# The last step of three expert stages, written out without the work for a next group of experts

## The chip, the cores and the metric

One core of a Trainium2 chip runs the whole program. The metric is the device time of one execution in microseconds (us), median of the runs. TensorE has a granted clock, 2.4 GHz at 1.0 and 1.2 GHz at 0.5 in the profile's column PEclk.

## The reference

256 tokens of width 1024 go through two blocks. The first has forgetting attention, a state-space branch and a mixture of experts; the second has two layers (a convolution or block attention, attention over a memory of 256 rows, and a mixture of experts each), with layer norms. The three mixtures are the stages e1, e2 and e3. Each has 32 experts, of which every token uses two; e1's experts are 256 wide, those of e2 and e3 512. The reference, cut to one mixture:

```python
def hierarchical_moe(x, w_rg, b_rg, w_re, b_re, w_gate, w_up, w_down):
    ...
    combine = (jax.nn.one_hot(g_idx, N_GROUPS, dtype=jnp.float32)[:, :, None]
               * within[:, None, :]).astype(t.dtype)
    out = jnp.zeros_like(t)
    for g in range(N_GROUPS):
        h = (jax.nn.silu(jnp.einsum('td,edf->tef', t, w_gate[g]))
             * jnp.einsum('td,edf->tef', t, w_up[g]))
        out = out + jnp.einsum('tef,efd->td', h * combine[:, g, :, None], w_down[g])
    return out.reshape(b_, s_, d_)
```

## The kernel before

A stage takes its experts in groups: four at a time in e1 (8 steps), two at a time in e2 and e3 (16 steps). The 128 columns of a matmul's token side are shared out among the experts of a group. A step of a group works like this, in the order of TensorE's program (`step_`, lines 1071 to 1181):

- The gate products, then the up products (line 1125), from `xg`, the gathered tokens of this group, and the weights as they arrive. `arrived` waits for a transfer of weights. In e2 and e3 each expert's matrix comes in two halves of 1 MB, so k = 4 and, for the down weights, f = 2 have a wait of their own; in e1 a matrix is one transfer of 1 MB.
- The gather of the next group's tokens, first half (line 1133, matmuls at line 1032 in e1 and 1045 in e2 and e3) against the one-hot matrix `S` that VectorE has made one step ahead.
- Four transposes (two in e1) of h (line 1136), which VectorE has multiplied together (line 2206) from ScalarE's SiLU (line 1622) and the up products in PSUM.
- The second half of the gather (line 1139), and two transposes of the shares `Sw` (line 1141).
- The down products (line 1164), once ScalarE has copied the turned h to `hT` (line 1626); the first product with f = 0 of each half also waits until the gather's bank has been copied out (`xgA`, ScalarE line 1591; `xgB`, VectorE line 2165), since it writes the same PSUM bank (4 or 7).
- The scatter (line 1177): shares times the result `og` (copied out by lines 1628 and 2213) is added to four banks that hold the sum over all groups.

VectorE makes `S` and `Sw` for the next group (`places` and `shares_of`, lines 2148 to 2163) at the start of its step. After the last group there is no next one; the kernel makes the one-hot, the shares and the gather all the same, for experts 32 and up, whose columns are filled so that they choose nobody, and nothing reads them. Two waits behind the last step (lines 1191 and 1192) see that these copies have ended.

In e1 all steps are written out, on every engine. In e2 and e3 TensorE and ScalarE have a loop of 8 rounds with two steps each; VectorE has its first and its last step outside of a loop of 7 rounds. Semaphores are counted up through all stages: `before_layer` adds what the stages before have counted, and for the five names that run one group ahead one step more per stage.

SyncE issues the weights on one queue: per step gate, up and down, each when the buffer is free (`used`). Behind a stage's last weights it issues the chunks that the next part of the program needs.

Of the kernel before, what the change touches and what calls it, by code (L numbers as in the profile page):

```python
# [38 lines left out]
GROUP = {"e1": 4, "e2": 2, "e3": 2}  # L39
# [59 lines left out]
def _build(ctx, nc, ins, out):  # L99
# [435 lines left out]
    def after(eng, who, name):  # L535

        eng.wait_ge(finished[who], milestones[who].index(name) + 1)
# [1 line left out]

    per_step = {"S": 2, "gathA": 1, "gathB": 1, "xgA": 1, "xgB": 1, "silu": 1, "h": 1, "T": 1, "hT": 1, "Sw": 1, "SwT": 1,  # L540
                "down": 1, "outA": 1, "outB": 1, "scattered_bank": 2, "scattered0": 1, "scattered": 1}
    ahead = ("S", "gathA", "gathB", "xgA", "xgB")

    def before_layer(e, name):

        return sum(per_step[name] * (STEPS[x] + (name in ahead)) for x in GROUP if x < e)


    SEED = 1
# [1 line left out]
    def moe_wait(eng, e, name, value):  # L551

        eng.wait_ge(flag("moe_" + name), value + (before_layer(e, name) + SEED))
# [264 lines left out]
    def _(pe):  # L818
# [135 lines left out]
        def moe(e, tok):  # L954
# [113 lines left out]
                                  start=(k == 0), stop=(k == KD - 1))  # L1068
                close_bank(last, "memv")

            def step_(u, i, keys=False, values=False):

                def c(k, per=1):

                    return i * (2 * per) + (u * per + k)
# [52 lines left out]
                            elif e != "e1" and k % 4 == 3 and n in (1, 3):  # L1128
                                last.then_inc(used[slots[X * g + (n == 1)][0] + k // 4], 1)

                moe_wait(pe, e, "S", c(4, 2))
                moe_wait(pe, e, "outA", c(0))
                gather_parts(1 - u, 0)
                moe_wait(pe, e, "h", c(1))
                for f in range(F):
                    last = pe.transpose(psum[:, 5, f * P:(f + 1) * P], hh[:, f * P:(f + 1) * P], ident[:, :])
                last.then_inc(flag("moe_T"), 1)
                moe_wait(pe, e, "outB", c(0))
                gather_parts(1 - u, 1)
                for th in range(TH):  # L1140
                    last = pe.transpose(psum[:, 6, th * P:(th + 1) * P], Sw[:, u, th, :], ident[:, :])
                last.then_inc(flag("moe_Sw"), 1)
# [5 lines left out]
                for fs, half in ([(range(F), 0), (range(F), 1)] if e == "e1" else  # L1148
                                 [((0, 1), 0), ((0, 1), 1), ((2, 3), 0), ((2, 3), 1)]):
                    if 0 in fs:  # L1150
                        moe_wait(pe, e, ("xgA", "xgB")[half], c(2))
                    elif half == 0:
                        for x in range(X):
                            arrived(2 * X + x, 1)
                    for f in fs:
                        for n in blocks:
                            r = slice(n * BLOCK, (n + 1) * BLOCK)
                            if e == "e1":
                                w = wv[n][:, f, half * 512:(half + 1) * 512]
                            elif n:  # L1160
                                w = wv[n == 1][:, f, half * 512:(half + 1) * 512]
                            else:
                                w = ring_flat[:, bass.ds(chosen + (4 * SLOT + f * D + half * 512), 512)]
                            last = mm(psum[r, (4, 7)[half], :], hT[:, f, r], w, start=(f == 0), stop=(f == F - 1))  # L1164
                            if half and f == fs[-1] and (e == "e1" or n in (1, 3)):
                                hs = slots[2 * X + (n if e == "e1" else n == 1)][0]
                                last.then_inc(used[hs + (f == 3)], 1)
                    if half == 0 and F - 1 in fs:
                        last.then_inc(flag("moe_down"), 1)
# [12 lines left out]

            if e == "e1":
                for n in range(STEPS[e]):
                    step_(n % 2, n // 2, n == KEYS_AT, n == VALUES_AT)
            else:
                with pe.Fori(0, STEPS[e] // 2) as i:
                    for u in range(2):
                        step_(u, i)

            moe_wait(pe, e, "xgA", STEPS[e] + 1)
            moe_wait(pe, e, "xgB", STEPS[e] + 1)


            ovp, ovv = flag(e + "_ovf_pe"), flag(e + "_ovf_vec")
            after(pe, "vec", e + "_items")
# [348 lines left out]
    def _(ac):  # L1545
# [38 lines left out]
        def moe(e):  # L1584
            S, Sw, SwT, xg, sg, hT = tiles[e]
            F = 2 if e == "e1" else 4
            FW = F * P
            X = GROUP[e]

            def gathered(par):  # L1590
                act(xg[:, par, 0:4, :], psum[:, 4, :].rearrange("p (k c) -> p k c", k=4), ACT.Copy).then_inc(flag("moe_xgA"), 1)  # L1591

            after(ac, "vec", e + "_gd")
            step(act(r_ge, r_gd, ACT.Exp))
            finish(ac, "act", e + "_ge")
            after(ac, "vec", e + "_d21")
            step(act(r_p2, r_d21, ACT.Exp))
            finish(ac, "act", e + "_p2")
            if e != "e1":
                for th in range(TH):  # L1600
                    step(act(parts[0][th], x_sb[:, th, :], ACT.Copy))
                finish(ac, "act", e + "_hi")
            if e != "e3":
                src = full(ac, e + "sums")
                copy_out((e + "sums",), wr_sums[:, :], src[:, 0:2 * NR])
            moe_wait(ac, e, "gathA", 1)
            gathered(0)
            if e == "e1":
                ac.dma_start(wr[:, :, :], ins["wr"][2]).then_inc(flag("router_w3"), 16)
            if e != "e1":  # L1610
                for th in range(TH):
                    after(ac, "vec", e + f"_rest{th}")
                    step(act(parts[1][th], rest[th], ACT.Copy))
                    finish(ac, "act", e + f"_mid{th}")
            def step_(u, i):

                def c(k, per=1):
                    return i * (2 * per) + (u * per + k)

                hs, per, at_u = last_half(e, u, X - 1)  # L1620
                ac.wait_ge(used[hs], i * per + (moe_used[e][hs] + at_u + 1 + SEED))
                act(sg[:, 0:FW], psum[:, 5, 0:FW], ACT.Silu).then_inc(flag("moe_silu"), 1)  # L1622
                moe_wait(ac, e, "gathA", c(2))
                gathered(1 - u)
                moe_wait(ac, e, "T", c(1))
                act(hT[:, 0:F, :], psum[:, 5, 0:FW].rearrange("p (f c) -> p f c", f=F), ACT.Copy).then_inc(flag("moe_hT"), 1)
                moe_wait(ac, e, "down", c(1))
                act(og[:, 0:512], psum[:, 4, :], ACT.Copy).then_inc(flag("moe_outA"), 1)  # L1628

            if e == "e1":  # L1630
                for n in range(STEPS[e]):
                    if n == KEYS_AT:
                        src = full(ac, "memk")
                        copy_out(("memk",), mem_k[:, :, :], src.rearrange("p (a t) -> p a t", a=2))
                    step_(n % 2, n // 2)
            else:
                with ac.Fori(0, STEPS[e] // 2) as i:
                    for u in range(2):
                        step_(u, i)
            after(ac, "vec", e + "_items")  # L1640
            n = ac.value_load(ovf[0:1, 2 * NOVF:2 * NOVF + 1], min_val=0, max_val=ITEMS[e])
            with ac.If(n > 0):
                with ac.Fori(0, n) as k_:
                    ac.wait_ge(flag(e + "_ovf_pe"), k_ * OVF_PE + (OVF_PE + 2))
                    act(sg[:, 0:FW], psum[:, 5, 0:FW], ACT.Silu).then_inc(flag(e + "_ovf_silu"), 1)
# [234 lines left out]
    def _(ve):  # L1880
# [194 lines left out]
        def moe(e):  # L2075
# [118 lines left out]
                    step(tt(parts[2][th], rest[th], parts[1][th], ALU.subtract))  # L2194
                tell(e + "_parts")

            def step_(u, n, i, first=False):

                places(1 - u, n + 1)
                shares_of(1 - u, n + 1)  # L2200
                if first and e != "e1":
                    thirds()
                hs, per, at_u = last_half(e, u, 2 * X - 1)
                ve.wait_ge(used[hs], i * per + (moe_used[e][hs] + at_u + 1 + SEED))
                moe_wait(ve, e, "silu", n + 1)
                tt(hh[:, 0:FW], sg[:, 0:FW], psum[:, 6, 0:FW], ALU.mult).then_inc(flag("moe_h"), 1)  # L2206
                moe_wait(ve, e, "gathB", n + 2)
                gathered(1 - u)
                moe_wait(ve, e, "Sw", n + 1)
                ve.tensor_copy(SwT[:, :], psum[:, 6, 0:T]).then_inc(flag("moe_SwT"), 1)  # L2210
                hs, per, at_u = last_half(e, u, 3 * X - 1)
                ve.wait_ge(used[hs], i * per + (moe_used[e][hs] + at_u + 1 + SEED))
                ve.tensor_copy(og[:, 512:1024], psum[:, 7, :]).then_inc(flag("moe_outB"), 1)  # L2213
# [32 lines left out]
            if e == "e1":  # L2246
# [8 lines left out]
                for n in range(1, STEPS[e]):  # L2255
                    if n == VALUES_AT:
                        src = full(ve, "memv")
                        read_out(ve.tensor_copy(mem_v[:, :, :], src.rearrange("p (a t) -> p a t", a=2)), "memv")
                    step_(n % 2, n, n // 2)
            else:  # L2260
                with ve.Fori(0, last) as i:
                    step_(1, i * 2 + 1, i)
                    step_(0, i * 2 + 2, i + 1)
                step_(1, STEPS[e] - 1, last)
            ovp, ovv = flag(e + "_ovf_pe"), flag(e + "_ovf_vec")
            n = ve.value_load(ovf[0:1, 2 * NOVF:2 * NOVF + 1], min_val=0, max_val=ITEMS[e])
            with ve.If(n > 0):
# [485 lines left out]
```

## Time and profile before

| | us |
|---|---|
| median of 3 runs | 1691.69 (1689.48 to 1695.86) |
| the profiled execution | 1690.12, of which the span of the instructions 1688.4 |
| TensorE busy | 1589.4 (94% of the span) |
| VectorE, ScalarE, GpSimd busy | 512.8, 276.6, 35.9 |
| mean granted clock of TensorE | 0.986 |
| moved by DMA | 570 MB, 338 GB/s on average |

By the page, the chain of work that ended last is 64% TensorE and 30% one tensor's transfers, the up weights (in_e_up). The busiest lines of TensorE are 1125 (520.5 us) and 1164 (257.2 us). e1 runs from about 245 to 470 us of the span, e2 from 597 to 1061, e3 from 1216 to 1680. A busy TensorE is not a TensorE at its peak, since the ends of matmuls are modelled; what decides is which wait ends last at each place. The rows below are times in us from the start of the span.

### The profile page before, as it was taken

The numbers are of one execution on the slowest core, as the hardware profiler recorded it, in microseconds if no ns is written. First come the engines' busy times: TensorE is split into PE (matmuls) and PEld (weight loads), VectorE is DVE, ScalarE is ACT, GpSimd is POOL, SyncE is SP. The second block draws the span as 40 slices with busy tenths as digits, with TensorE's granted clock in tenths as the row PEclk, the third lists the DMA queues.
The fourth block names the chain that finished last, engine by engine and source line by source line (L and its number), as shares of the span: only waits on it lengthen the run. The fifth ranks groups of instructions, "written<-read, shape, count | busy, mean of one in ns | idle before, by whom it ended". The sixth has DMA issues, their size and how long they took to land.

```text
span 1688.4 us, 30942 instructions
## 1 busy us (share of the span) xinstructions
PE 1589.4 (94%) x12616; PEld 795.9 (47%) x12620; DVE 512.8 (30%) x1162; ACT 276.6 (16%) x549; POOL 35.9 (2%) x78
## 2 busy tenths in 40 slices
PE   7999999876799999999999999999999999999997
PEld 5487765533467544343433333674543434333332
DVE  7994333110157551111111111414631111111113
ACT  2304120000035221000100100214210100010011
POOL 4000000100000000000000000000000000000000
PEclk9999999988899999999999999999999999999999
DMA  6322769999983289999999999841399999999996
GB/s 253 139 112 72 319 253 415 421 421 421 422 334 134 76 347 422 422 421 422 422 422 422 422 422 424 353 148 53 150 391 421 422 422 422 422 422 421 422 422 262
DMA packets 79529, 570.25 MB, mean 338 GB/s; under 512 B 8879, under 2 KB 12391, under 8 KB 14567
## 3 DMA queue, kind: packets, MB, share of 16 engines
q1 hardware_dynamic: 77750, 563.41, 81.4%
q10 hardware_dynamic: 1712, 5.92, 0.9%
q8 instruction: 47, 0.77, 0.2%
q14 instruction: 20, 0.16, 0.0%
HBM read 568.24 MB, written 1.05 MB: 337 GB/s over the span
## 4 chain that ended last, share of the span: by engine, by line
PE 64%; DMA 30%; DVE 2%; ACT 1%; issue 1%; SPq 1%; DVEq 0%; ACTq 0%
DMA space<-in_e_up 30%; PE psum L1125 20%; PE psum L1164 8%; PE psum L850 6%; PE psum L913 6%; PE psum L858 5%; PE psum L1177 4%; PE psum L1045 3%; PE psum L1493 2%; PE psum L1453 1%; PE psum L1253 1%; PE psum L1032 1%; PE psum L891 1%; PE psum L1504 1%; PE psum L1393 1%
## 5 line engine op out<-in xcount | busy, mean ns | idle before, releaser
L1125 PE MATMUL psum<-space 128*32 128x512 f32 (+2 forms) x4992 | 520.5, 566 | 51.2 <-DMA space<-in_e_up 46.4
L1125 PEld LDWEIGHTS psum<-space 128*32 128x32 f32 x4992 | 166.8, 113 | 391.7 <-issue 383.0
L1164 PE MATMUL psum<-space 128*32 128x512 f32 (+1 forms) x2304 | 257.2, 597 | 5.9 <-DMA space<-in_e_down 5.8
L2206 DVE TENSOR_TENSOR space<-space,psum 128x512 f32<-128x512 f32 (+1 forms) x40 | 25.4, 634 | 578.6 <-PE psum L1125 578.6
L1177 PE MATMUL psum<-space 128*128 128x512 f32 x320 | 150.3, 613 | 0.0
L1164 PEld LDWEIGHTS psum<-space 128*32 128x32 f32 x2304 | 72.2, 110 | 161.6 <-issue 161.6
L1177 PEld LDWEIGHTS psum<-space 128*128 128x128 f32 x320 | 54.2, 189 | 96.6 <-issue 71.8
L2213 DVE COPY space<-psum 128x512 f32<-128x512 f32 x40 | 27.7, 692 | 231.1 <-PE psum L1164 231.1
L1622 ACT ACTIVATE space<-psum 128x512 f32<-128x512 f32 (+1 forms) x40 | 22.2, 554 | 412.5 <-PE psum L1125 412.5
L1045 PE MATMUL psum<-space,xT 128*128 128x128 bf16 x1024 | 89.4, 219 | 0.0
L850 PE MATMUL psum<-xT,space 128*128 128x256 f32 x384 | 85.2, 381 | 3.1 <-ACT xT L1557 1.0
L1591 ACT ACTIVATE space<-psum 128x512 f32<-128x512 f32 x43 | 25.7, 597 | 354.2 <-PE psum L1045 266.4
L1045 PEld LDWEIGHTS psum<-space,xT 128*128 128x128 bf16 x1024 | 68.0, 98 | 27.2 <-issue 26.8
L850 PEld LDWEIGHTS psum<-xT,space 128*128 128x128 f32 x384 | 72.3, 190 | 14.6 <-issue 5.1
L913 PE MATMUL psum<-xT,space 128*128 128x256 f32 x320 | 74.1, 384 | 0.0
L1045 PE MATMUL psum<-space,PT_buf 128*128 128x128 bf16 x512 | 70.3, 219 | 0.0
L913 PEld LDWEIGHTS psum<-xT,space 128*128 128x128 f32 x320 | 59.1, 190 | 11.5 <-issue 4.1
L2165 DVE COPY space<-psum 128x512 f32<-128x512 f32 x43 | 29.7, 692 | 109.6 <-PE psum L1045 77.1
L1628 ACT ACTIVATE space<-psum 128x512 f32<-128x512 f32 x40 | 23.9, 597 | 233.3 <-PE psum L1164 233.3
L858 PE MATMUL psum<-space,xT 128*128 128x512 f32 (+1 forms) x128 | 49.0, 541 | 0.2 <-PE psum L1280 0.2
L1045 PEld LDWEIGHTS psum<-space,PT_buf 128*128 128x128 bf16 x512 | 39.3, 98 | 0.0
L1032 PE MATMUL psum<-space 128*128 128x128 f32 x288 | 35.8, 278 | 1.0 <-DVE space L2158 1.0
(407 smaller groups left out, 1414.3 us busy)
## 6 DMA issues: line engine op xcount, KB each, us to landing
space<-in_e_up SPq DMA_DIRECT2D x160, 1024.0 KB, 20.4
space<-in_e_down SPq DMA_DIRECT2D x160, 1024.0 KB, 20.5
space<-in_e_gate SPq DMA_DIRECT2D x152, 1024.0 KB, 20.9
space<-in_stream SPq DMA_DIRECT2D x25, 2048.0 KB, 14.5
rows<-in_e_gate SPq DMA_DIRECT2D x4, 1024.0 KB, 25.4
x_sb<-in_e_gate SPq DMA_DIRECT2D x4, 1024.0 KB, 26.6
rows<-in_rows ACTq DMA_DIRECT2D x8, 512.0 KB, 8.1
space<-in_stream SPq DMA_DIRECT2D x3, 1024.0 KB, 9.6
```

The lines of the kernel that those rows point to most:

```text
L850: last = mm(psum[:, b, n * T:(n + 1) * T], w[:, k, c * P:(c + 1) * P], rhs[:, k, :], start=(k == 0), stop=(k == K - 1))
L858: last = mm(psum[:, b, 0:c1 - c0], lhs[:, k0 + k, th * P:(th + 1) * P], w[:, k, c0:c1], start=(start and k == 0), stop=(stop and k == K - 1))
L913: last = mm(psum[:, b, n * T:(n + 1) * T], w[:, k, c * P:(c + 1) * P], rhs[:, k, :], start=(k == 0), stop=(k == K - 1))
L1032: last = mm(psum[:, (4, 7)[half], k * P:(k + 1) * P], tok[:, th, (4 * half + k) * P:(4 * half + k + 1) * P], S[:, par, th, :], start=(th = ...
L1045: last = mm(psum[:, (4, 7)[half], k * P:(k + 1) * P], parts[n][th][:, cols], S_half[:, par, th, :], start=(n == 0 and th == 0), stop=(n == ...
L1125: last = mm(psum[r, 5 + g, 0:FW], xg[:, u, k, r], w, start=(k == 0), stop=(k == KD - 1))
L1164: last = mm(psum[r, (4, 7)[half], :], hT[:, f, r], w, start=(f == 0), stop=(f == F - 1))
L1177: last = mm(psum[:, 2 * th + half, :], SwT[:, th * P:(th + 1) * P], og[:, half * 512:(half + 1) * 512], start=False, stop=False, skip_grou ...
L1493: return mm(psum[:, b, :], yT[:, k, th * P:(th + 1) * P], w[:, k % 4, hf * 512:(hf + 1) * 512], start=not started, stop=(k == MT - 1))
L1591: act(xg[:, par, 0:4, :], psum[:, 4, :].rearrange("p (k c) -> p k c", k=4), ACT.Copy).then_inc(flag("moe_xgA"), 1)
L2165: ve.tensor_copy(xg[:, par, 4:8, :], psum[:, 7, :].rearrange("p (k c) -> p k c", k=4)).then_inc(flag("moe_xgB"), 1)
L2213: ve.tensor_copy(og[:, 512:1024], psum[:, 7, :]).then_inc(flag("moe_outB"), 1)
```

## The change

The last step of every stage gets `final=True` and leaves out what is for a next group: on VectorE `places`, `shares_of` and the copy of the gather's second half, on ScalarE the copy of its first half, on TensorE the wait for `S`, both halves of the gather, and the waits for `xgA` and `xgB` in the down products. To have a last step of its own, TensorE and ScalarE run 7 rounds of the loop in e2 and e3 instead of 8, and two steps are written out behind it. The two waits behind the last step and the step more per stage in `before_layer` are gone. In all steps TensorE's wait for `S` now stands behind the one for `outA`. Gate, up and down products, their weights and SyncE's program are the same.

```diff
-    ahead = ("S", "gathA", "gathB", "xgA", "xgB")
-
     def before_layer(e, name):
 
-        return sum(per_step[name] * (STEPS[x] + (name in ahead)) for x in GROUP if x < e)
+        return sum(per_step[name] * STEPS[x] for x in GROUP if x < e)
...
-                moe_wait(pe, e, "S", c(4, 2))
                 moe_wait(pe, e, "outA", c(0))
-                gather_parts(1 - u, 0)
+                if not final:
+                    moe_wait(pe, e, "S", c(4, 2))
+                    gather_parts(1 - u, 0)
                 moe_wait(pe, e, "h", c(1))
...
                 moe_wait(pe, e, "outB", c(0))
-                gather_parts(1 - u, 1)
+                if not final:
+                    gather_parts(1 - u, 1)
...
                     if 0 in fs:
-                        moe_wait(pe, e, ("xgA", "xgB")[half], c(2))
+                        if not final:
+                            moe_wait(pe, e, ("xgA", "xgB")[half], c(2))
...
-                    step_(n % 2, n // 2, n == KEYS_AT, n == VALUES_AT)
+                    step_(n % 2, n // 2, n == KEYS_AT, n == VALUES_AT, n == STEPS[e] - 1)
             else:
-                with pe.Fori(0, STEPS[e] // 2) as i:
+                last_i = STEPS[e] // 2 - 1
+                with pe.Fori(0, last_i) as i:
                     for u in range(2):
                         step_(u, i)
-
-            moe_wait(pe, e, "xgA", STEPS[e] + 1)
-            moe_wait(pe, e, "xgB", STEPS[e] + 1)
-
+                step_(0, last_i)
+                step_(1, last_i, final=True)
...
-                moe_wait(ac, e, "gathA", c(2))
-                gathered(1 - u)
+                if not final:
+                    moe_wait(ac, e, "gathA", c(2))
+                    gathered(1 - u)
...
-                with ac.Fori(0, STEPS[e] // 2) as i:
+                last_i = STEPS[e] // 2 - 1
+                with ac.Fori(0, last_i) as i:
                     for u in range(2):
                         step_(u, i)
+                step_(0, last_i)
+                step_(1, last_i, final=True)
...
-                places(1 - u, n + 1)
-                shares_of(1 - u, n + 1)
+                if not final:
+                    places(1 - u, n + 1)
+                    shares_of(1 - u, n + 1)
...
-                moe_wait(ve, e, "gathB", n + 2)
-                gathered(1 - u)
+                if not final:
+                    moe_wait(ve, e, "gathB", n + 2)
+                    gathered(1 - u)
```

## Rows read from the trace of the kernel before

**Rows 1.** Chain of waits in e2 (start, us, what): two early, two late steps

```profile
740.49 13.87 PE psum L1125 x128
...
768.50 13.87 PE psum L1125 x128
...
983.30 3.66 PE psum L1125 x31
...
1013.00 3.66 PE psum L1125 x31
```

**Rows 2.** DMA queues from 710 to 1043 us (packets, MB, share); no other queue

```profile
q1 hardware_dynamic: 19291, 140.48, 101.3%
```

**Rows 3.** Chain of waits, end of e3

```profile
1635.92 25.65 DMA space<-in_e_up
...
1661.70 3.64 PE psum L1125 x32
1665.34 1.45 PE psum L1045 x24
1666.79 0.44 PE psum L1136 x4
1667.23 1.34 PE psum L1045 x24
...
1668.79 7.00 PE psum L1164 x64
```

**Rows 4.** Timeline, end of e3 (start, us, engine, line, operation, idle before)

```profile
1665.43 0.69 DVE L2206 TENSOR_TENSOR space<-space,psum 128x512 f32<-128x512 f32 x1 [16.56 <-PE psum L1125]
...
1667.32 0.59 ACT L1626 ACTIVATE space<-psum 128x512 f32<-128x512 f32 x1
...
1668.72 7.07 PE L1164 MATMUL psum<-space 128*32 x64
```

**Rows 5.** Timeline, end of e1

```profile
458.14 0.42 DVE L2206 TENSOR_TENSOR space<-space,psum 128x256 f32<-128x256 f32 x1 [21.01 <-PE psum L1125]
...
459.82 0.38 PE L1136 MATMUL psum<-ident,space 128*128 128x128 f32 x2
...
462.13 3.64 PE L1164 MATMUL psum<-space 128*32 128x512 f32 x32
```

**Rows 6.** Last down weights of e3, e2, e1: issue times, then us to landing

```profile
L635 SPq DMA_DIRECT2D space<-in_e_down x2: 328/575/822, 1646.0 to 1646.4; - x2
DMA to landing us min/median/max: 23.0/24.1/25.1
...
L635 SPq DMA_DIRECT2D space<-in_e_down x4: 328/380/1481, 1023.7 to 1027.5; - x4
DMA to landing us min/median/max: 21.5/23.3/25.1
...
L640 SPq DMA_DIRECT2D space<-in_e_down x2: 430/430/430, 436.4 to 436.8; - x2
DMA to landing us min/median/max: 22.6/23.6/24.6
```

**Rows 7.** Timeline, end of e2

```profile
1049.97 7.07 PE L1164 MATMUL psum<-space 128*32 x64
```

**Rows 8.** Who SyncE's queue waited for (us, times, longest)

```profile
SPq L635 <- PE psum L1493: 49.2, 1, 49.2
SPq L635 <- PE psum L1453: 46.6, 1, 46.6
```

**Rows 9.** DMA queues from 271 to 451.6 us, six steps of e1

```profile
q8 instruction: 11, 0.18, 0.4%
```

**Rows 10.** Earlier e1 steps that waited for down weights; last, busy and clock by window

```profile
311.04 3.64 PE L1164 MATMUL psum<-space 128*32 128x512 f32 x32 [2.16 <-DMA space<-in_e_down]
...
340.93 5.34 PE L1164 MATMUL psum<-space 128*32 128x512 f32 x32 [2.25 <-DMA space<-in_e_down]
...
340.90:344.30 3.40, 3.38 (x20) 1.18 (x24) 0.00 (x0) 0.00 (x0) 0.00 (x0) 0.54 1.02 424
```

More of the change, by code:

```diff
@@ L1069, in memory_values, with step_ @@
                 close_bank(last, "memv")
-            def step_(u, i, keys=False, values=False):
+            def step_(u, i, keys=False, values=False, final=False):
                 def c(k, per=1):
@@ L1614, in moe, with step_ @@
                     finish(ac, "act", e + f"_mid{th}")
-            def step_(u, i):
+            def step_(u, i, final=False):
                 def c(k, per=1):
@@ L1634, in moe @@
                         copy_out(("memk",), mem_k[:, :, :], src.rearrange("p (a t) -> p a t", a=2))
-                    step_(n % 2, n // 2)
+                    step_(n % 2, n // 2, n == STEPS[e] - 1)
             else:
-                with ac.Fori(0, STEPS[e] // 2) as i:
+                last_i = STEPS[e] // 2 - 1
+                with ac.Fori(0, last_i) as i:
                     for u in range(2):
                         step_(u, i)
+                step_(0, last_i)
+                step_(1, last_i, final=True)
             after(ac, "vec", e + "_items")
@@ L2195, in thirds, with step_ @@
                 tell(e + "_parts")
-            def step_(u, n, i, first=False):
-                places(1 - u, n + 1)
-                shares_of(1 - u, n + 1)
+            def step_(u, n, i, first=False, final=False):
+                if not final:
+                    places(1 - u, n + 1)
+                    shares_of(1 - u, n + 1)
                 if first and e != "e1":
@@ L2258, in moe @@
                         read_out(ve.tensor_copy(mem_v[:, :, :], src.rearrange("p (a t) -> p a t", a=2)), "memv")
-                    step_(n % 2, n, n // 2)
+                    step_(n % 2, n, n // 2, final=n == STEPS[e] - 1)
             else:
@@ L2263, in moe @@
                     step_(0, i * 2 + 2, i + 1)
-                step_(1, STEPS[e] - 1, last)
+                step_(1, STEPS[e] - 1, last, final=True)
             ovp, ovv = flag(e + "_ovf_pe"), flag(e + "_ovf_vec")
```

## The prediction

> **What bounds the kernel now.** I read the chain of waits first, then the timeline around the last step of each expert stage, then the landing times of that step's weights. The three expert stages (e1: 8 steps, e2 and e3: 16 steps each) read 12 transfers of 1 MB a step. Where TensorE sets the pace a step of e2 takes 768.50 - 740.49 = 28.0 us; where the weights do it takes 1013.00 - 983.30 = 29.7 us [rows 1]. The queue runs at one rate throughout: 140.48 MB in the 333 us from 710 to 1043, 422 GB/s [rows 2]. So e2 and e3 begin at TensorE's pace, use up their lead, and end at the pace of the weights. e1's later steps also wait for weights. The change touches nothing of the loads, so no more can be gained inside a stage; only its last step can shorten, and there only the part behind the last arriving weights.
>
> The end of e3 [rows 3]: the last "up" half lets the last gate/up products start at 1661.70; they end at 1665.34. Then TensorE gathers the first half of a pair that nobody uses (1.45 us), turns h (0.44 us), gathers the second half (1.34 us), turns the shares (0.22 us by the gap that is left) and starts the down products at 1668.79. Those last 7.00 us, then the scatter (line 1177), the norm and the stores. The rows of e2's end have the same form with the same durations. The chain names no DMA behind 1661.70, which looks as if the whole 2.79 us of gathering were on the path. It is not, for two reasons.
>
> **The change part by part.**
>
> *First reason: h.* The down products need hT, which comes from VectorE's product (starts 1665.43, 0.69 us, ends 1666.12), four transposes and ScalarE's copy (0.59 us) [rows 4]. Today TensorE gathers meanwhile. Without the gather: transposes from about 1666.2 to 1666.85, copy from 1666.95 (hand-over 0.1 us, as from 1667.23 to 1667.32 today [rows 3, 4]) to 1667.55, down products from about 1667.6. Against 1668.72 that is 1.1 us for e3 and the same for e2, not 2.8. In e1 the product ends at 458.14 + 0.42 = 458.56, the two transposes take 0.38, the copy at most 0.59; the down products could start at about 459.65 instead of 462.13, 2.5 us earlier [rows 4, 5]. If nothing else held them the sum would be 2.5 + 1.1 + 1.1 = 4.7 us.
>
> *Second reason: the down weights.* They are issued last and land last, and they take over the wait. In e3 the last transfer is issued at 1646.4 and lands 25.1 us later, at 1671.5 [rows 6]. It holds rows f = 2, 3 of the product, the second half of the 7.07 us, which TensorE reaches at 1668.72 + 3.45 = 1672.17 [rows 4]. From landing to first product takes 0.13 us (up: issued 1635.92, 25.65 us on the way, product 1661.70 [rows 3]). So it can start at 1671.63 at the earliest: e3 gains 1672.17 - 1671.63 = 0.54 us, and the other 0.6 becomes a wait for "down" in the middle of line 1164. In e2: 1027.5 + 25.1 + 0.13 = 1052.73 against 1049.97 + 3.45 = 1053.42, so 0.69 us [rows 6, 7]. In e1 all four down weights are awaited before the first down product: 436.8 + 24.6 + 0.13 = 461.53 against 462.13, so 0.60 us [rows 5, 6]. The sum is 1.83 us. All landing times are rounded to 0.1 us, so each is good to 0.1.
>
> *Does a gain in e1 or e2 live on?* The loads of e2 stop for 46.6 us, those of e3 for 49.2 us, until TensorE has come to the out-projection or the attention before that stage [rows 8]. So the start of the next run of loads moves with TensorE, and with it the stage's end. The chain between the stages holds only compute. I count both gains in full.
>
> *Removed from VectorE and ScalarE.* The one-hot and the shares of the last round (four operations) and two copies out of PSUM. VectorE waits for line 1125 through most of a step; its one-hot work begins after the copy of line 2213, while TensorE scatters and multiplies with older weights. It is worth nothing, and if that cover were gone at most the four operations, 2.2 us (as 0.69 each for two and 0.42 for two, estimated from rows of the same shapes [rows 4, 5]), once a stage. The moved wait on "S" in all other steps: what it waits for was made a step before; nothing. The two final waits on "xgA" and "xgB": their copies are over some 6 us before; nothing. No wait is added, the transfer order on SP's queue is the same, and ScalarE's loop for one pair less costs its few instructions.
>
> *Added: code.* TensorE's and ScalarE's last two steps of e2 and e3 are written out behind the loop. The trace has no code of e2's last steps to fetch, so I bound it by e1, whose steps are all written out: 11 instruction packets, 0.18 MB, for six steps [rows 9]. By the counts of the recorded matmuls an e1 step has 128 + 32 + 4 + 32 + 8 = 204 of them, each with its load of weights; a step of e2 has 128 + 48 + 6 + 64 + 8 = 254, and the last one now 206 [rows 1, 3]. So the added code is about 4 packets or 70 KB a stage: at 422 GB/s 0.17 us of a queue that has been full since the stage began. It lands before the last weights and delays them. Bounds: nothing (if fetched while loads stand still, as at the stage's start), and 0.6 us a stage, if a 16 KB packet holds one of 16 DMA engines and every weight transfer waits for it (16 KB at 422/16 GB/s = 0.62 us, for packets that fall on one another's engine; all four on one would be 2.5). I take 0.17, since e1's steps, with these packets in them, waited no longer than those of e2.
>
> *The sum.* -0.60 (e1) - 0.69 + 0.17 (e2) - 0.54 + 0.17 (e3) = -1.5 us. The profiled execution took 1690.12 us (span 1688.4 and 1.7 around it); it becomes 1688.6. It is 1.57 us below the median of the runs shown, and the step from before to after is what I predict, so from the median 1691.69 I come to 1690.2.
>
> **The rivals.**
>
> *Slower, by the clock.* After the change TensorE in e1 has 0.6 us of transposes between 457.9 and 461.5, and stands idle for its last 2.1 or so, waiting for "down". The same wait at the same line is in the trace twice: idle 2.16 us before 311.04, and the down products took 3.64 us; idle 2.25 us before 340.93, and they took 5.34 us, at a granted clock of 0.54 in the 3.4 us from 340.9, the lower level of 1.2 GHz for most of it [rows 10]. The price is 1.70 us, more than e1's 0.60 and enough to turn the total into +0.2 us, 1691.9. It decides whether the clock is still at 2.4 GHz when the down products start. One of two such waits lost it; before this one TensorE was sparser still.
>
> *Slower, by the code.* Today no instruction packet comes between 710 and 1043, through more than ten steps of the loop [rows 2]: the loop's code stays. If with the longer code behind it the loop were fetched anew each round, that would be 14 rounds of some 4 packets, 0.9 MB or 2.2 us, and a stop S at each jump back. TensorE has 2 x 1.7 = 3.4 us to spare a round [rows 1], so up to there it costs 2.2 - 1.8 = +0.4 us, and beyond that 14 x (S - 3.4): at S = 4 it is 9 us, 1700.5. Against it: e2 today also has the next stage's code behind its loop.
>
> The Trainium skill has the rule behind this rival ("Runtime: NRT & Kernel Launch", Instruction fetch mechanics): code is prefetched in sequence in blocks of 16 KiB, and a taken branch to a target that is no longer held forces a fetch before execution goes on. It speaks against any change that makes the code behind a loop longer. Today's trace shows no such fetch in 333 us.
>
> *The weights are not last.* If the last transfers land earlier than the rounded rows say, or the 0.13 us doesn't apply, each stage gains its full 2.5, 1.1 and 1.1 us: 1691.7 - 4.7 + 0.3 = 1687.3. Against it: three separate landing times, each within 0.7 us of the use.
>
> *Nothing comes through.* Code packets at the upper bound, 0.6 us a stage, leave 1.83 - 1.2 = 0.6 us: 1691.1.
>
> **How the numbers follow.** Forecast, -1.5 us at full clock: 0.48. Clock lost in e1, +0.2: 0.30. Nothing through: 0.10. Full gains: 0.07. Loop refetched: 0.03, part of it above 0.5%. Rest 0.02. All but the code rival lie within 5 us of before. A measurement here tells about 0.5% or 8.5 us from no change, and the runs shown spread over 6.4 us by themselves (1689.48 to 1695.86). So: faster by more 0.02, within 0.95, slower by more 0.03. Range: from the full gains, 1687.3, to the clock and the refetch without long stops, about 1692.5, and around them a part of the runs' own spread, which is larger than any term of my sum: 1686.5 to 1695.0.
>
> **What would show it.** In the profile after: the last steps have no line for the gather. In e1's last step the down products wait for in_e_down, start near 461.5 (on e1's own clock of before) and take 3.6 us, or 5.3 if the clock fell. In e2 and e3 they start 1.1 us earlier behind the last gate/up product (about 2.3 us after its end instead of 3.4), and pause some 0.5 us for in_e_down in their middle. The loops show no instruction packets; four or so more come in each of e2 and e3. I am wrong if down products run through without a wait (full gains), if the steps in the loop get longer than 28.0 or 29.8 us (code), or if the sections between the stages don't shift as a whole.

## The result, and the profile after

Beside each other on one chip, nine executions each: 1691.69 us median before (1688.06 to 1695.86), 1700.6 us after (1690.39 to 1703.42). The ratio is 1.004 with a 95% interval of 1.0023 to 1.0057: the change makes the kernel 0.4% slower. The forecast was 1690.2 us in a range of 1686.5 to 1695.0, so both the direction and the range were wrong. Three further comparisons gave 1.0036, 1.0025 and 1.0033.

The profiled execution of after, however, is the fastest of its nine, 1690.39 us, and its span of 1688.7 us is within 0.3 us of before's 1688.4. It cannot show a loss of 5 us or more; it shows whether the parts of the sum are there. The head of its page (the third line is for the instruction fetches of all engines; before's page counts 47 packets of 0.77 MB there):

```profile
span 1688.7 us, 30582 instructions
...
PE 1584.1 (94%) x12491; PEld 788.7 (47%) x12492; DVE 505.9 (30%) x1149; ACT 272.6 (16%) x544; POOL 35.4 (2%) x78
...
q8 instruction: 55, 0.90, 0.2%
```

In the kernel after, line 1123 is the gate/up product (before: 1125), 1135 the transposes of h (1136), 1165 the down product (1164), 1178 the scatter (1177). Timeline at the end of e3 (start, us, engine, line, operation, idle before), which answers to rows 3 and 4:

```profile
1662.72 3.64 PE L1123 MATMUL psum<-space 128*32 x32 [1.48 <-DMA space<-in_e_up]
1667.29 0.63 PE L1135 MATMUL psum<-ident,space 128*128 128x128 f32 x4 [0.92 <-DVE space L2211]
1667.75 0.38 PE L1141 MATMUL psum<-ident,space 128*128 128x128 f32 x2
1668.69 7.38 PE L1165 MATMUL psum<-space 128*32 x64 [0.56 <-ACT space L1627]
```

The gather is gone. From the end of the gate/up product (1666.36 by this view) to the first down product are 2.3 us, where before had 3.4. The down product takes 7.38 us instead of 7.07, since TensorE pauses in it. In e2 the pause names its cause (timeline, answers to rows 7):

```profile
1047.80 3.19 PE L1165 MATMUL psum<-space 128*32 x28
1051.34 3.64 PE L1165 MATMUL psum<-space 128*32 x32 [0.34 <-DMA space<-in_e_down]
```

And the chain of waits, which named no DMA at this place before, now runs through the last down weights:

```profile
1026.10 25.00 DMA space<-in_e_down
1051.10 0.24 issue
1051.34 3.64 PE psum L1165 x32
```

At the end of e1, which answers to rows 5 (timeline):

```profile
456.70 0.38 PE L1141 MATMUL psum<-ident,space 128*128 128x128 f32 x2
459.73 3.64 PE L1165 MATMUL psum<-space 128*32 128x512 f32 x32 [2.66 <-DMA space<-in_e_down]
```

TensorE waits 2.66 us for the down weights and in this execution keeps its clock: 3.64 us. Last, the queue in the middle of e2's loop, 710 to 970 us, which answers to rows 2. It is the only queue there; no instruction packet comes:

```profile
q1 hardware_dynamic: 15064, 109.69, 101.3%
```

So every mechanism of the sum is visible, and the kernel is slower all the same. One execution of each could not settle this: the same two kernels, profiled again, gave spans of 1697.1 us (after) and 1695.4 us (before). The experiments therefore work in two ways. The timed comparisons say how much each part of the change costs, and the profiles, 18 of them over all kernels, say what happens where and, roughly, how often.

### The profile page after: what moved, and what is told of

Its sections match the earlier page's. It is cut to its first block, busy times and chain, and to the rows that moved or that the text cites. A ratio compares the mean times of both kernels' runs of the same rounds, so it can differ in the third digit from the quotient of the medians.

```text
span 1688.7 us, 30582 instructions
## 1 busy us (share of the span) xinstructions
PE 1584.1 (94%) x12491; PEld 788.7 (47%) x12492; DVE 505.9 (30%) x1149; ACT 272.6 (16%) x544; POOL 35.4 (2%) x78
## 4 chain that ended last, share of the span: by engine, by line
PE 56%; DMA 33%; DVE 7%; issue 2%; ACT 1%; SPq 1%; POOL 0%; DVEq 0%; ACTq 0%; POOLq 0%
DMA space<-in_e_up 21%; PE psum L1123 17%; DMA space<-in_e_down 11%; PE psum L1165 9%; PE psum L911 6%; PE psum L1178 4%; PE psum L848 3%; PE psum L1043 3%; PE psum L856 2%; PE psum L1493 2%; DVE space L2416 1%; PE psum L1453 1%; PE psum L983 1%; PE psum L1030 1%; PE psum L889 1%
## 5 line engine op out<-in xcount | busy, mean ns | idle before, releaser
L1043 PE MATMUL psum<-space,xT 128*128 128x128 bf16 x960 | 83.8, 219 | 0.0
L1043 PEld LDWEIGHTS psum<-space,xT 128*128 128x128 bf16 x960 | 63.7, 98 | 25.5 <-issue 25.1
L1043 PE MATMUL psum<-space,PT_buf 128*128 128x128 bf16 x480 | 66.0, 219 | 0.0
L1572 ACT ACTIVATE rows<-rows,small 128x256 f32<-128x256 f32 (+1 forms) x56 | 25.8, 462 | 59.1 <-DVE small L1960 59.0
```

The source lines that it names most:

```text
L1043: last = mm(psum[:, (4, 7)[half], k * P:(k + 1) * P], parts[n][th][:, cols], S_half[:, par, th, :], start=(n == 0 and th == 0), stop=(n == ...
L1572: act(P_buf[:, k, 0:W], P_buf[:, k, 0:W], ACT.Exp, bias=nmax[:, k:k + 1], accum_out=psums[:, k:k + 1]).then_inc(flag("attn_exp"), 1)
```

## The experiments

Unless a sentence says otherwise, times are medians, and ratios are to the kernel before on the same chip. "Pooled" is the mean over all executions of one kernel in all comparisons after the first, plus or minus its standard error (differences too); for after its nine first ones are in too. Before, pooled: 1692.8 +- 0.3 us, 116 executions.

**The change again, three times.** No edit.

> The changed kernel once more, unchanged. Its nine times so far lie in two groups, 1690.4 and 1691.5 against seven from 1698.2 to 1703.4, and its one profile is of the low group, so no profile shows where the 9 us are. Theory code (the two steps written out behind the loops of e2 and e3 make TensorE stop for code in most executions): again most times near 1700, and a profile of such a time has a stop of several us at the loop's exit or at its jump back. Theory clock (TensorE's clock falls more often, since the last steps leave gaps): most times near 1700, and a profile has lower clock in e1. If the groups were only chance of that chip: times of 1688 to 1696 as before the change.

> The changed kernel, in the same rounds and on the same chip as the filled ones: ratio 1.003 to 1.005 by its 19 times so far, whatever the theory. Its profile is a third sample: clock: down products of e1 at 5 us or more where the time is near 1700, 3.6 us where it is near 1691.

> The whole change in the same rounds: 1.0025 to 1.004 again. If the parts add up, it is e1_only's ratio plus e23_only's. A fourth profile of it, read for the two events seen so far: down products of e1 at the lower clock, and a stop of TensorE of 1 to 2.3 us that waits for nothing, behind e1's last scatter.

Measured: 1698.73 us, ratio 1.0036 (1.0015 to 1.0057); 1697.65, 1.0025 (1.0007 to 1.0043); 1697.15, 1.0033 (1.0016 to 1.0049). Pooled over 42 executions 1698.1 +- 0.6: the change costs 5.3 +- 0.7 us. Timeline at the end of e1 in the first of these:

```profile
460.06 6.42 PE L1165 MATMUL psum<-space 128*32 128x512 f32 x32 [2.33 <-DMA space<-in_e_down]
```

The same 32 products that took 3.64 us above take 6.42, behind a wait of 2.33 us. The columns of the next view are stretch, length and busy time of PE, PEld, DVE, ACT and POOL, then the granted clock, the DMA share and GB/s:

```profile
457.00:460.00 3.00, 0.63 (x4) 0.42 (x4) 0.42 (x1) 0.38 (x1) 0.00 (x0) 0.81 1.06 448
460.00:463.40 3.40, 3.34 (x16) 0.92 (x20) 0.00 (x0) 0.00 (x0) 0.00 (x0) 0.50 1.01 429
463.40:466.80 3.40, 3.40 (x21) 0.99 (x14) 0.18 (x1) 0.60 (x1) 0.00 (x0) 0.66 0.98 419
```

TensorE is busy for 0.63 us in the 3 us before the down products; then it runs at the lower of its two clocks, 1.2 GHz (0.50), for the first 3.4 us and for part of the next. That is the rival of the clock that the prediction named. After_fourth shows it too:

```profile
459.91 6.57 PE L1165 MATMUL psum<-space 128*32 128x512 f32 x32 [2.19 <-DMA space<-in_e_down]
```

After_third kept its clock (2.69 us of waiting, then 3.64). The length of the wait thus does not decide it: the clock was kept behind 2.66 and 2.69 us and lost behind 2.33 and 2.19. No run shows what does.

**Only e1's part.** e2 and e3 are as in the kernel before; all work that e1's last step needs is there.

This diff, like the next ones up to the last experiment, is against the kernel after and is cut to TensorE's part; the loop has its 8 rounds again.

```diff
+FINAL = ("e1",)
+WRITTEN_OUT = ()
...
-                with pe.Fori(0, last_i) as i:
+                with pe.Fori(0, last_i + (e not in WRITTEN_OUT)) as i:
...
-                step_(0, last_i)
-                step_(1, last_i, final=True)
+                if e in WRITTEN_OUT:
+                    step_(0, last_i)
+                    step_(1, last_i, final=e in FINAL)
```

> Only e1's last step leaves out the work for a next group; e2 and e3 are as before, in whole loops. Theory code: like before, within 0.2%, all times from 1688 to 1696. Theory clock (the fall is in e1's last step or behind it): two groups, most times near 1700. My prediction's own sum for this part: -0.6 us, or +1.1 if the clock falls once.

> e1's part alone once more, for its size: 1.0008 with an interval from 0.9992 to 1.0025 so far. Theory clock in e1: 1.001 to 1.003, and the larger part of the whole change's 1.003. Its profile: down products of e1 at 5.3 us or more if the clock fell (so far in this kernel once of one, in the whole change once of three).

> e1's part alone, in the same rounds as the two above: 1.001 to 1.003 by its 22 times so far (3.2 us over before on average). Theory clock: above the two others; down products at 5.3 us or more in four of five profiles.

Measured: 1693.76, ratio 1.0008 (0.9992 to 1.0025); 1697.03, 1.0027 (1.0008 to 1.0047); 1699.74, 1.0066 (1.0042 to 1.0089, six executions). The three scatter more than their intervals suggest; pooled over 28 executions 1697.5 +- 0.8, +4.6 +- 0.9 us. All three profiles show the clock lost. The timeline of the first:

```profile
463.33 5.34 PE L1169 MATMUL psum<-space 128*32 128x512 f32 x32 [3.28 <-DMA space<-in_e_down]
```

The others have 5.34 us behind 3.29 and 3.38 us of waiting.

**Only the part of e2 and e3.** e1 is as before.

```diff
+FINAL = ("e2", "e3")
+WRITTEN_OUT = ("e2", "e3")
...
-                    step_(n % 2, n // 2, n == KEYS_AT, n == VALUES_AT, n == STEPS[e] - 1)
+                    step_(n % 2, n // 2, n == KEYS_AT, n == VALUES_AT, e in FINAL and n == STEPS[e] - 1)
```

> e1 as before; e2 and e3 as in the change (written out, and the last step without the gather, one-hot and shares). Theory code: like the whole change, most times near 1700. Theory clock in e1: like before.

> e2's and e3's part alone once more: 1.0011, interval 0.9995 to 1.0028 so far. By the profiles it should gain 0.5 us a stage less 0.1 to 0.3 for code, 0.9995; theory clock in e1 has nothing against that. If it stays at 1.001 or more, there is a loss in these stages that no profile has shown.

Measured: 1695.46, 1.0011 (0.9995 to 1.0028); 1693.63, 1.0012 (0.9997 to 1.0028). Pooled over 22 executions 1694.65 +- 0.6, +1.8 +- 0.7 us. With e1's +4.6 that makes +6.4 +- 1.1 against the whole change's +5.3 +- 0.7: the parts add up within the error, and most of the loss lies in e1. With e1's gather in place, e1's down products wait little and keep the clock (timeline of e23_only):

```profile
462.73 3.64 PE L1169 MATMUL psum<-space 128*32 128x512 f32 x32 [0.63 <-DMA space<-in_e_down]
```

**Only the writing out.** e2 and e3 have their last two steps behind the loop, but those still gather, make the one-hot and the shares, and wait, as before.

```diff
+FINAL = ()
+WRITTEN_OUT = ("e2", "e3")
...
-                step_(0, last_i)
-                step_(1, last_i, final=True)
+                if e in WRITTEN_OUT:
+                    step_(0, last_i)
+                    step_(1, last_i, final=e in FINAL)
```

> The last two steps of e2 and e3 are written out on TensorE and ScalarE, but every step still does all the work for a next group. Theory code: most times near 1700, as for the whole change. Theory clock or gaps: like before, 1688 to 1696, since no gap in TensorE's work is new.

Measured: 1693.93, 1.0008 (0.9988 to 1.0027), not told apart from nothing; nor, at 1694.3 +- 1.2 in the mean of ten, from e23_only's 1694.65. In the profile e2 and e3 take 446.5 us each from the start of the first gate product to the end of the last up product (before: 446.2 and 446.0).

**All of e2 and e3 written out.** To weigh the code's price, I multiplied it: all 16 steps of both stages without a loop, all work kept.

```diff
-                with pe.Fori(0, last_i) as i:
-                    for u in range(2):
-                        step_(u, i)
-                step_(0, last_i)
-                step_(1, last_i, final=True)
+                for n in range(STEPS[e]):
+                    step_(n % 2, n // 2)
```

> All 16 steps of e2 and of e3 written out on TensorE and ScalarE, no loop left there; every step does all its work. That is eight times the written-out code of the change, some 30 more instruction packets a stage. Theory code, steady (each packet holds up the weights): the profiles put a written-out step with packets at 29.82 to 29.97 us against 29.82, so at most 0.1 us a step, 3 us in all; if the 1.3 us of the two written-out steps were real and all theirs, eight times as much, some 10 us, ratio 1.006. Theory clock: no new gaps in TensorE's work, ratio 1.000 to 1.001.

Measured: 1703.13, 1.0064 (1.0044 to 1.0083), some 10 us slower, though the mean granted clock is no lower than before's (0.9850 over its six executions, 0.9841 over before's 116). The fetches on its page, and below it the queues from 710 to 1043, the stretch of rows 2:

```profile
q8 instruction: 107, 1.75, 0.4%
```

```profile
q1 hardware_dynamic: 19171, 139.62, 100.8%
q8 instruction: 24, 0.39, 0.5%
```

Where rows 2 have 140.48 MB of data and no code, here are 139.62 MB and 24 packets. Chain of waits, steps of e2 that wait for weights:

```profile
839.44 3.66 PE psum L1127 x31
869.34 3.66 PE psum L1127 x31
899.65 3.66 PE psum L1127 x31
930.43 3.66 PE psum L1127 x31
960.24 3.66 PE psum L1127 x31
990.10 3.66 PE psum L1127 x31
1020.42 3.66 PE psum L1127 x31
```

The steps take 29.8 to 30.8 us, 30.16 in the mean ((1020.42 - 839.44) / 6). The same chain of the kernel before has 29.83 in the mean of its last six ((1042.95 - 864.00) / 6):

```profile
864.00 3.66 PE psum L1125 x31
...
1042.95 3.64 PE psum L1125 x32
```

No stop of TensorE over 0.2 us in either stage is without a named cause; it only waits longer for weights. From the first gate product to the end of the last up product e2 and e3 take 452.6 and 450.9 us, 11.2 us more than before, for 58 packets more (34 and 33 against 5 and 4): 0.19 us a packet. By the data alone it would be less: 0.86 MB are missing for 24 packets, at 422 GB/s 2.0 us or 0.08 us each. The rest would fit transfers that land late because one of the 16 engines was held by code, which is argued from the uneven steps and not shown. By either figure a packet costs two to five times what its 16 KB take of the 422 GB/s (0.04 us).

**Work in the gap, first amounts.** In e1's last step TensorE does 3 products with a tile of zeros in place of the first half of the gather and 9 in place of the second (fill_e1); fill_all adds 4 and 2 in e2's and e3's last step. The rest is the whole change. The zeros go into banks that the next product starts anew.

```diff
                 if not final:
                     gather_parts(1 - u, 0)
+                elif e in FILL:
+                    idle_products(4, FILL[e][0])
```

> As the one before, with the products of zeros in e1's last step alone. If the clock's fall at e1's end is what costs, this is as good as filling all three: ratio within 0.1% of it. If the short waits in e2 and e3 cost as much, it lies half way to the whole change. Theory code: like the whole change, 1.003 to 1.005.

> The whole change, but where the last steps dropped the gather TensorE does products of zeros that nobody reads, only as many as fit the waits: in e1 3 of 128x512 in bf16 in place of the first half and 9 in place of the second, in e2 and e3 4 and 2 (0.21 us each). Theory clock (the waits in the last steps, above all the one for the down weights in e1, let TensorE's clock fall, and down products, scatter and what follows pay): the group near 1700 is gone, median at or below before's, ratio 0.998 to 1.001; in e1's last step the down products take 3.6 us. Theory code (stops for instructions): no better than the whole change, ratio 1.003 to 1.005.

Measured: 1694.37, 1.0016 (0.9997 to 1.0035), and 1697.05, 1.0024 (1.0009 to 1.004). Pooled 1695.6 +- 1.1 and 1697.3 +- 1.0, together 1.7 +- 1.0 us below the whole change: a hint, no more. Both profiles kept e1's clock; fill_all waited 1.40 us, fill_e1 (timeline):

```profile
459.93 3.64 PE L1174 MATMUL psum<-space 128*32 128x512 f32 x32 [0.46 <-DMA space<-in_e_down]
```

Filling e2's and e3's shorter gaps bought nothing that shows. The expected 0.998 to 1.001 for fill_all did not come: it is as slow as the whole change within the error, although e1's down products have the full clock in its profile. They may thus not be the only place where time is lost.

**TensorE keeps its gather in e1.** As e1_only, so VectorE and ScalarE drop the one-hot, the shares and the copies, and the waits are gone; but TensorE still does the 16 products of each half. They read the one-hot of an earlier step, and nobody reads what they give.

```diff
                 if not final:
                     gather_parts(1 - u, 0)
+                else:
+                    idle_gather(1 - u, 0)
```

> e1's part alone, but TensorE does its gather in e1's last step as before (of the one-hot that is still there; nobody reads the result); the one-hot, the shares, the two copies and the waits for them are left out. Theory clock (it is the gap in TensorE's work that costs e1's part its 3 us): like before, ratio 0.999 to 1.001, down products of e1 at 3.6 us. If what costs lies with the other engines or the counts of the semaphores: 1.002 as e1's part alone.

**The gap filled in full.** As e1_only, with 9 and 9 products of zeros.

> e1's part alone, with 9 products of zeros (128x512, bf16) in place of each half of the gather, 1.9 us each as the gather took. Theory clock: as the one before, ratio 0.999 to 1.001 and 3.6 us for the down products. If products of zeros don't hold the clock as the gather does: 1.002, and 5 to 6 us in its profile.

Measured in one comparison, beside e1_only_3 with its 1.0066: e1_keep_pe 1694.24, ratio 1.0014 (0.9995 to 1.0033); e1_fill_full 1693.24, 1.0012 (0.9997 to 1.0028). Pooled over both kernels, 24 executions, 1694.3 +- 0.8: 3.2 +- 1.2 us below e1_only. Without the six executions of e1_only_3, which are the slowest of its kind (1701.9 in the mean), the difference is 2.0 +- 1.2. So a good part of e1's loss, by the pooled numbers two thirds of it, comes from TensorE's gap itself, and useless products of either kind take that part away; what the other engines leave out in e1 does not bring it. The timelines, e1_keep_pe first:

```profile
462.70 3.64 PE L1181 MATMUL psum<-space 128*32 128x512 f32 x32 [0.38 <-DMA space<-in_e_down]
```

```profile
462.59 3.64 PE L1174 MATMUL psum<-space 128*32 128x512 f32 x32 [0.17 <-DMA space<-in_e_down]
```

**The kernel before again, and its own starts filled.** No edit in the first. In the second 3 products of zeros more stand ahead of the first gather of e2, and 9 where there were 5 ahead of e3's.

```diff
+            if e == "e2":
+                idle_products(1, 3)
...
-                idle_products(0, 5)
+                idle_products(0, 9)
```

> The kernel before, for a second profile of it. Theory clock: the down products of e1's last step run at the full clock (3.6 us) with TensorE busy from the last up product to them, whatever the total is. Its 31 times on this chip spread from 1688.4 to 1698.3, so falls of the clock elsewhere, at the starts of e1, e2 and e3, cost it up to 8 us too; a high time here should show them there.

> The kernel before with more products of zeros ahead of the first gather: 3 more in e2 and 4 more in e3, in waits of TensorE of 0.7 and 1.5 us. Nothing else is changed. Its own falls of the clock lie there (the first gather of e1, e2 and e3 took 5.3 to 5.7 us instead of 3.8 in a profile of 1697 us). If filling short waits holds the clock: 0.998 to 1.000, mean clock above 0.984. If it doesn't, 1.000 to 1.001, for the products then only come on top.

Measured: before_again has a span of 1695.4 us, and the first gather of e1, e2 and e3 takes 5.4, 5.4 and 5.8 us in it, where it takes 3.8 each time in the first profile of before. The kernel before thus loses its clock at its stages' starts in some executions. Over its 116 executions a mean granted clock lower by 0.001 goes with 1.2 us more, so the clock is a large part of its own spread (1686.7 to 1699.5 us). Starts_filled gave 1692.85, 1.0001 (0.9989 to 1.0013). Its mean clock is 0.9855, against 0.9847 of the kernel before beside it, as expected if filling holds the clock, but it is no faster. No version found here beats the kernel before.

## Why the prediction was wrong

**The clock in e1: the step that failed.** The sum took e1's down products at the full clock behind the new wait, 3.64 us, and so a lost clock at nothing; the prediction saw the place, the wait and a price (1.70 us, from the wait before 340.93 in rows 10), but as a rival with a chance of 0.30. "One of two such waits lost it; before this one TensorE was sparser still": that pointed at more than one in two. Of the seven profiles in which e1's last step has neither gather nor filling, five show down products of 5.34 to 6.57 us; of the eleven others none does, all have 3.64. The price was also too small: 2.8 and 2.9 us were lost where the lower clock lasted into a second stretch, 1.70 in the other three, so 2.2 us where it happened and 5/7 x 2.2 = 1.6 us on average. The case of that rival was the likeliest, and its total not +0.2 us but +0.7 by this price.

**The gain in e1.** Forecast 0.60 us. From the end of e1's last up product to the first down product, kernels without e1's gather have 3.5 to 4.0 us where before has 4.1. In the eleven profiles where e1's first gather took 5.4 us instead of 3.8 they have 4.6 to 4.7, and before and its like 4.7 to 4.9. The gain is thus 0.35 us in the mean of the first kind and 0.2 in that of the second, some 0.25 in all. In the second kind the down products waited 0.4 to 0.7 us for their weights with the gather in place too. The one profile on which the 0.60 was worked out had no such wait.

**e2 and e3: the h chain and the down weights.** Right, in every profile that has this part of the change. The way from the end of the last up product to the first down product fell from 3.4 to 2.3 us (forecast 1.1 less), and the down products grew from 7.07 us to between 7.4 and 7.6 (forecast: a pause of some 0.5). About 0.55 us a stage stay, against 0.69 and 0.54 in the sum.

**The code.** The loop stays held, as forecast: no packet from 710 to 970, so the longer code behind it did not make the loop be fetched anew. The packets were counted rightly too: the page has 55 for 47, and from 590 to 1055 us there are 9 where there were 5. Their price was mis-sized: 0.04 us each in the sum (0.17 for four), 0.08 to 0.19 by out_all, so 0.3 to 0.8 us a stage. The stages' gate/up parts agree: 446.6 us in e2 and 447.2 in e3 as the mean of nine profiles with written-out last steps, against 446.3 and 446.8 for eight with the whole loop, 0.3 and 0.5 us more. That lies inside the prediction's own upper bound of 0.6. So e2 and e3 together come to -1.1 + 0.8 = -0.3 us by their profiles, not -0.9.

**A stop that was not in the list.** In three of the eleven profiles with e1's part, TensorE stops for 2.27, 2.62 and 4.60 us at the transposes of the next section and goes on some 8 us after e1's down products. It waits for nothing that the view names. After_again (timeline):

```profile
470.50 1.72 PE L836 MATMUL psum<-ident,x_sb 128*128 128x128 f32 x14 [0.30 <-DVEq L533]
474.50 0.44 PE L836 MATMUL psum<-ident,x_sb 128*128 128x128 f32 x2 [2.27 <-issue]
```

E1_fill_full, whose down products had the full clock:

```profile
474.54 3.65 PE L841 MATMUL psum<-ident,x_sb 128*128 128x128 f32 x16 [4.60 <-issue]
```

Behind this stop the clock is down as well: the 16 transposes take 3.65 us, where they take 1.94 in e1_keep_pe, and the view by windows has the lower clock for 10 us (columns as above):

```profile
473.40:480.20 6.80, 4.67 (x19) 4.15 (x20) 1.46 (x4) 2.48 (x3) 0.65 (x2) 0.50 1.01 426
480.20:483.60 3.40, 3.40 (x10) 2.68 (x9) 0.00 (x0) 0.00 (x0) 0.00 (x0) 0.50 1.02 434
```

So a stop costs more than its length. From the end of e1's last up product to e2's first gate product after_again takes 151.1 us, e1_only_3 151.1 and e1_fill_full 151.7; their nearest relatives without a stop (after_fourth, e1_only, e1_keep_pe) take 145.5, 146.8 and 146.8. That is 4.9 us a stop on average. What is lost there stays lost: after_again begins e2 at 607.5 us and e3 at 1227.9, after's first profile at 598.4 and 1218.4.

In before and in after's first profile an instruction packet lands at about 463 us and the next at 472 to 474. In the three with the stop the first of these is missing, and one comes only as TensorE stands: after_again has it between 471.5 and 474 (queue view).

```profile
q8 instruction: 1, 0.02, 2.7%
```

That fits code fetched too late, which no run tests. The Trainium skill ("Runtime: NRT & Kernel Launch", Instruction fetch mechanics) says that straight code is fetched ahead and that crossing a block's edge is mostly hidden. Out_all agrees as far as TensorE goes, which stops for none of its 60 packets more, and shows a price elsewhere, 0.08 to 0.19 us a packet in later weights. The three stops of 2.3 to 4.6 us, if they are for code, speak against it. Why the packet is late in one execution and not in the next, of one and the same kernel, no run shows; e1_only and e1_only_2 have it at about 471 us without a stop. None of the seven profiles without e1's part has such a stop or so late a packet; with 3 stops in 11, that is no proof that e1's part brings them.

**What stays open.** By the profiles e1's part costs 1.6 (clock) + 3/11 x 4.9 = 1.3 (stop) - 0.25 (gain) = about 2.7 us. The whole stretch from e1's last up product to e2's first gate product says much the same: 146.7 us in the mean of the seven profiles with neither gather nor filling, 144.3 in the seven that have e1 as before, a difference of 2.3 +- 1.4. The timed runs say 4.6 +- 0.9, which so few profiles do not contradict. In the four filled kernels the stretch has 146.8 us (one has the stop of 4.60), so the gain by filling rests on the timed runs alone. For the whole change the profiles are also too kind: its four profiled executions have spans of 1691.3 us in the mean, all 42 have 1696.4.

The granted clock is on record for every execution, profiled or not, and says more:

| kernel | executions | mean, us | mean granted clock |
|---|---|---|---|
| before | 116 | 1692.8 | 0.9841 |
| after | 42 | 1698.1 | 0.9820 |
| e1_only | 28 | 1697.5 | 0.9820 |
| e1_keep_pe and e1_fill_full | 24 | 1694.3 | 0.9834 |
| e23_only | 22 | 1694.7 | 0.9840 |

Among executions of one kernel, 0.001 less of clock goes with 1.2 us (before), 1.5 (e1_only) or 1.7 (after). The 0.0021 that after and e1_only lack thus go with 2.5 to 3.6 us, about half or more of their 5.3 and 4.6. This is a correlation: it does not say where in the program the clock fell, and a stop for another reason lowers the clock behind it too. Together with the filled kernels it makes a lower clock, begun by TensorE's gap in e1, the likely largest part of the loss; how much of it is not shown more closely. The part of e2 and e3 is -0.3 us by its profiles and +1.8 +- 0.7 by the timed runs, and its clock is before's, so that loss is not the clock's. The code written out is the rival left (out_only, which has nothing else, has +1.5 +- 1.2), and it is not shown.

**The range.** It failed because its upper end was the clock's smallest price with a little code (1692.5) and a part of the runs' spread. The three events that were listed with a price, clock, code and the lost gain, all lie on the slow side. Taken together at the listed prices they reach 1691.7 + 1.7 + 1.2 = 1694.6 without any spread, and 1695.8 with the 2.9 us of clock that the runs showed. That is still under the 1698.1 us of the kernel after; the stop was not in the list.

## What to carry to other kernels

Dead work on an engine that waits for a transfer anyway can cost very little (0.25 us in e1, 0.55 a stage in e2 and e3), and in e1 it was worth more than that: with it TensorE kept its clock for the products behind. Before taking it out, ask what the engine does in the microseconds ahead of its next long piece, and if the same wait has already lost the clock once in the trace, count that as the likely case. A change whose expected gain is below the kernel's own spread needs its parts timed with twenty or more executions each (ten gave +- 1.2 us here); the profile of one execution confirms mechanisms, not their frequency, and the clock of every timed execution shows what few profiles miss.

## What the runs showed of the hardware

- Behind waits of 2.2 to 3.4 us, with 0.6 us of transposes ahead of them, e1's down products took 5.34 to 6.57 us instead of 3.64 in five of seven profiles. In the eleven profiles with the gather or products of zeros there (waits of at most 1.40 us) they took 3.64. In after_again TensorE ran at 0.50 for the first 3.4 us of them and at 0.66 over the next.
- 60 instruction packets more in two stages bound by their weights cost some 10 us, though together they are 1 MB of 570.
- The kernel before, unchanged, gave spans of 1688.4 and 1695.4 us in two profiles; its first gathers take 3.8 us in one and 5.4 to 5.8 in the other. Over all profiles e1's first gate product starts at 246.6 to 248.4 us where its first gather took 3.8, and at 248.2 to 250.1 where it took 5.4.
- Behind a stop of 4.60 us TensorE ran at 0.50 for some 10 us (e1_fill_full).
